# Token-form products over 512 columns of weights instead of 256, in a transformer kernel on one NeuronCore

## The reference

```python
proj = h @ w_in[l]                       # of it: hi, the values of the recurrence
x = x + g1 * (concat([o_a, o_b, o_c]) @ w_out[l])
# second block, layer i
h = x @ w_in                             # of it: c_q, c_kv and the values of attention
x = layer_norm(DEEPNORM_ALPHA * x + mix @ w_out, ln1_g[i], ln1_b[i])
x = layer_norm(DEEPNORM_ALPHA * x + swiglu(x, ...), ln2_g[i], ln2_b[i])
x = x + sigmoid(x @ ple_w_gate[i] + ple_b_gate[i]) * (p[i] @ ple_w_proj[i])
```

## Time and profile before

| | |
|---|---|
| median of 3 runs | 1397.43 us (1397.06 to 1399.79) |
| the profiled execution | 1398.54 us, of which the span 1396.7 us |
| TensorE busy | 1190.8 us, 85% of the span, 8196 matmuls |
| VectorE busy | 767.4 us, 55% |
| ScalarE busy | 531.9 us, 38% |
| bytes read | 198.70 MB, 143 GB/s over the span |

### The profile page before, as it was taken

How to read it: one execution, slowest core, us unless ns; L and a number is a source line. 1 busy time by engine, 2 the same in 40 slices (tenths; PEclk the granted TensorE clock), 3 DMA queues, 4 the chain that set the end, 5 groups by cost and what they waited for, 6 DMA issues and landing times.

```text
span 1396.7 us, 19126 instructions
## 1 busy us (share of the span) xinstructions
PE 1190.8 (85%) x8196; PEld 1078.1 (77%) x8196; DVE 767.4 (55%) x969; ACT 531.9 (38%) x705; POOL 0.2 (0%) x4
## 2 busy tenths in 40 slices
PE   4889872847999997975879999977999889999966
PEld 2788871437999886973679998867987589999866
DVE  3652459255777435547475665465443466666374
ACT  4541311143443333356443333333454443333332
POOL 0000000000000000000000000000000000000000
PEclk7799987768999998997799999989999889999988
DMA  9430323802455554420125555524531034555530
GB/s 387 188 136 30 109 103 121 352 10 91 159 183 188 195 185 168 169 93 1 50 105 183 185 188 193 183 67 183 189 121 61 5 141 150 187 183 181 186 116 31
DMA packets 28275, 200.97 MB, mean 144 GB/s; under 512 B 3104, under 2 KB 3616, under 8 KB 5024
## 3 DMA queue, kind: packets, MB, share of 16 engines
q1 hardware_dynamic: 26624, 190.30, 37.2%
q10 hardware_dynamic: 1568, 9.46, 1.8%
HBM read 198.70 MB, written 1.05 MB: 143 GB/s over the span
## 4 chain that ended last, share of the span: by engine, by line
PE 71%; DVE 16%; ACT 6%; DMA 4%; issue 3%; DVEq 0%; SPq 0%; ACTq 0%
PE bank L523 21%; PE bank L528 20%; PE bank L529 20%; DMA raw<-wstream 4%; DVE w_lo L1363 3%; PE bank L675 2%; PE bank L712 2%; DVE hT_lo L1381 2%; PE bank L668 1%; DVE hT_hi L1380 1%; PE bank L921 1%; PE bank L920 1%; PE bank L603 1%; DVE x_res L1826 1%; ACT w_hi L1013 1%
## 5 line engine op out<-in xcount | busy, mean ns | idle before, releaser
L1363 DVE TENSOR_TENSOR w_lo<-raw,w_hi 128x2048 fp32r<-128x2048 f32 (+1 forms) x159 | 357.9, 2257 | 180.0 <-ACT w_hi L1013 170.5
L1013 ACT ACTIVATE w_hi<-raw 128x2048 fp32r<-128x2048 f32 (+1 forms) x159 | 299.8, 1886 | 356.3 <-PE bank L523 304.3
L523 PE MATMUL bank<-hT_hi,w_hi 128*128 128x256 f32 (+1 forms) x1360 | 393.5, 289 | 22.0 <-DVE w_lo L1363 17.2
L528 PE MATMUL bank<-hT_lo,w_hi 128*128 128x256 f32 (+1 forms) x1360 | 390.4, 287 | 0.0
L529 PE MATMUL bank<-hT_hi,w_lo 128*128 128x256 f32 (+1 forms) x1360 | 389.9, 287 | 0.0
L523 PEld LDWEIGHTS bank<-hT_hi,w_hi 128*128 128x128 f32 (+1 forms) x1360 | 265.2, 195 | 27.2 <-DVE w_lo L1363 18.7
L528 PEld LDWEIGHTS bank<-hT_lo,w_hi 128*128 128x128 f32 (+1 forms) x1360 | 265.3, 195 | 0.2
L529 PEld LDWEIGHTS bank<-hT_hi,w_lo 128*128 128x128 f32 (+1 forms) x1360 | 265.1, 195 | 0.2
L523 PE MATMUL bank<-w_hi,hT_hi 128*128 128x256 f32 (+2 forms) x544 | 161.8, 297 | 31.3 <-DVE w_lo L1363 19.2
L528 PE MATMUL bank<-w_lo,hT_hi 128*128 128x256 f32 (+2 forms) x544 | 159.5, 293 | 0.0
L529 PE MATMUL bank<-w_hi,hT_lo 128*128 128x256 f32 (+2 forms) x544 | 159.1, 292 | 0.0
(11 more groups left out here) (252 smaller groups left out, 1080.6 us busy)
## 6 DMA issues: line engine op xcount, KB each, us to landing
raw<-wstream SPq DMA_DIRECT2D x179, 1024.0 KB, 4.8
arena<-prow ACTq DMA_DIRECT2D x2, 2560.0 KB, 11.2
x_res<-x ACTq DMA_DIRECT2D x1, 1024.0 KB, 15.2
rows<-prow ACTq DMA_DIRECT2D x2, 512.0 KB, 23.8
out<-x_res SPq DMA_DIRECT2D x1, 1024.0 KB, 4.0
const_sb<-const ACTq DMA_DIRECT2D x1, 872.0 KB, 19.3
raw<-wstream SPq DMA_DIRECT2D x1, 768.0 KB, 4.5
raw<-wstream SPq DMA_DIRECT2D x1, 544.0 KB, 3.8
```

Of the source, the lines that this page charges most:

```text
L523: ins = mm(o, a[0], b[0], start=start, stop=False)
L528: mm(o, a[0], b[1], start=False, stop=False)
L1013: A(w_hi[n % HI][:, 0:m], raw[:, slot % RAW, 0:m], ACT.Copy).then_inc(weights_rounded, 1)
L1363: V.tensor_tensor(w_lo[slot][:, 0:m], raw[:, slot, 0:m], w_hi[n % HI][:, 0:m].bitcast(F32), ALU.subtract).then_inc(weights_split, 1)
```

## The change

For hi, wo0, wo1, cqkv, sbv, fv0, o and pg the two tiles of a product are cut another way. Each now holds 512 rows of weights (four chunks k) by all 512 columns: tile .0 holds k 0 to 3, tile .1 k 4 to 7. The data in device memory stay as they were, and each transfer picks two runs of 1024 floats per partition, one from either old tile. Each matmul streams 512 columns, in two runs of 256 that lie 1024 apart. Block t of tokens has bank t to itself, and both banks are filled over both tiles: block 0 and block 1 over tile .0, then block 0 (bank 0 is then full) and block 1 over tile .1. `pp` also streams 512 columns, with a block of tokens to each bank. fv1, sv and kr stay.

Whoever empties a bank now takes 512 columns of one block in place of 256 columns of both. `add_attention` takes one statistic after each bank, where it took two after every second.

```diff
+WIDE = ["hi", "wo0", "wo1", "cqkv", "sbv", "fv0"] + [f"{n}{i}_{j}" for n in ("o", "pg") for i in range(2) for j in range(2)]
...
+                if name[:-2] in WIDE:
+
+                    j = int(name[-1])
+                    a, b = (TILE_NO[name[:-1] + c] for c in "01")
+                    sp.dma_start(raw[:, i % RAW, :].rearrange("p (j n) -> p j n", j=2),
+                                 wstream[a:b + 1:b - a, :, j * 1024:(j + 1) * 1024].rearrange("j p n -> p j n"))\
+                        .then_inc(weights_loaded[i % RAW], 16)
...
             def gemm_token(name):
 
+
+                banks = [begin(name, t) for t in range(TT)]
                 for j in range(2):
-                    token_half(f"{name}.{j}", T, key=(name, j))
+                    wh, wl, first = tile(f"{name}.{j}")
+                    vh, vl = (w.rearrange("p (c k n) -> p k c n", c=2, k=4) for w in (wh, wl))
+                    for t in range(TT):
+                        for i in range(4):
+                            k = 4 * j + i
+                            x_ready(k)
+                            last = product3(banks[t][:, :], x_part(k, t * P, (t + 1) * P),
+                                            (vh[:, i, :, :], vl[:, i, :, :]), k == 0, k == DC - 1, first)
+                        if j == 1:
+                            last.then_inc(psum_full, 1)
...
-                for n_ in range(4):
-                    b = begin("pp", layer, n_)
+                for n_ in range(2):
                     for t in range(TT):
+                        b = begin("pp", layer, 2 * n_ + t)
                         for k in range(2):
...
-                    xs = x[:, :, q * T:(q + 1) * T]
-                    done(V.scalar_tensor_tensor(out=xs, in0=xs, scalar=ALPHA,
-                                                in1=b[:, :].rearrange("p (t n) -> p t n", t=2),
+                    xs = x[:, q % 2, q // 2 * 512:(q // 2 + 1) * 512]
+                    done(V.scalar_tensor_tensor(out=xs, in0=xs, scalar=ALPHA, in1=b[:, :],
                                                 op0=ALU.mult, op1=ALU.add), *key)
-                    if q % 2:
-                        for t in range(TT):
-                            last = bn_piece(t, q // 2)
+                    last = bn_piece(q % 2, q // 2)
```

More of the change, by code:

```diff
@@ L487, in _ @@
                         sp.wait_ge(psum_full, full("mod", int(before[3:]) // 2))
-                sp.dma_start(raw[:, i % RAW, 0:width(name)], wstream[i, :, 0:width(name)])\
-                    .then_inc(weights_loaded[i % RAW], 16)
+                if name[:-2] in WIDE:
[4 more added lines that the diff above has]
+                        .then_inc(weights_loaded[i % RAW], 16)
+                else:
+                    sp.dma_start(raw[:, i % RAW, 0:width(name)], wstream[i, :, 0:width(name)])\
+                        .then_inc(weights_loaded[i % RAW], 16)
             sp.wait_ge(x_done, 1)
@@ L939, in _ @@
                 pe.wait_ge(p_split, layer + 1)
-                for n_ in range(4):
-                    b = begin("pp", layer, n_)
+                for n_ in range(2):
                     for t in range(TT):
+                        b = begin("pp", layer, 2 * n_ + t)
                         for k in range(2):
                             a = k * T + t * P
-                            last = product3(b[:, t * T:(t + 1) * T], (hid2_hi[:, a:a + P], hid2_lo[:, a:a + P]),
-                                            (vh[:, k, n_ * T:(n_ + 1) * T], vl[:, k, n_ * T:(n_ + 1) * T]),
+                            last = product3(b[:, :], (hid2_hi[:, a:a + P], hid2_lo[:, a:a + P]),
+                                            (vh[:, k, n_ * 512:(n_ + 1) * 512], vl[:, k, n_ * 512:(n_ + 1) * 512]),
                                             k == 0, k == 1, first)
-                    last.then_inc(psum_full, 1)
+                        last.then_inc(psum_full, 1)
                 for i in range(2):
@@ L1190, in _ @@
                         b = bank_of(f"cqkv.{e}", "cqkv", e)
-                        A(xn[:, :, e * T:(e + 1) * T], b[:, :].rearrange("p (t n) -> p t n", t=2), ACT.Copy)
-                        for t in range(TT):
-                            last = A(xn[:, t, 512 + e * T:512 + (e + 1) * T], b[:, t * T:(t + 1) * T], ACT.Square,
-                                     accum_out=ssum[:, 2 * t + e:2 * t + e + 1])
+                        A(xn[:, e, 0:512], b[:, :], ACT.Copy)
+                        for i in range(2):
+                            last = A(xn[:, e, 512 + i * T:512 + (i + 1) * T], b[:, i * T:(i + 1) * T], ACT.Square,
+                                     accum_out=ssum[:, 2 * e + i:2 * e + i + 1])
                         done(last, "cqkv", e)
@@ L1205, in _ @@
                         b = bank_of(f"sbv.{j}", "sbv", j)
-                        done(A(v_b.rearrange("p (t n) -> p t n", t=2)[:, :, j * T:(j + 1) * T],
-                               b[:, :].rearrange("p (t n) -> p t n", t=2), ACT.Copy), "sbv", j)
+                        done(A(v_b[:, j * 512:(j + 1) * 512], b[:, :], ACT.Copy), "sbv", j)
                     for j in range(2):
@@ L1286, in fox_input @@
                             c = half * 512 + j * T
-                            done(A(v_c.rearrange("p (t n) -> p t n", t=2)[:, :, c:c + T],
-                                   b[:, :].rearrange("p (t n) -> p t n", t=2), ACT.Copy), n_, j)
+                            if half == 0:
+                                done(A(v_c[:, j * D:j * D + 512], b[:, :], ACT.Copy), n_, j)
+                            else:
+                                done(A(v_c.rearrange("p (t n) -> p t n", t=2)[:, :, c:c + T],
+                                       b[:, :].rearrange("p (t n) -> p t n", t=2), ACT.Copy), n_, j)
                         else:
```

25 lines of the change are left out of this document (11 added, 14 removed).

## The result

Over 20 runs each, the changed kernel took a median of 1406.68 us (1395.14 to 1410.65) and the kernel before 1398.38 us (1395.23 to 1405.28). The ratio is 1.0054, with a 95% interval of 1.0040 to 1.0068: slower by half a per cent, 12.7 us above the forecast of 1394.0 and outside its range. The runs of the changed kernel lie in two groups, 17 at 1405.5 to 1410.7 and three at 1395.1, 1401.5 and 1402.8. The profiled one took 1405.49 us, span 1403.7; the profiled one of before had a span of 1396.7.

A forecast was written before the change was run, and what follows sets the result against it. TensorE's stream of products was taken as the bound, three `product3` lines being 61% of the last chain. Gains of 7.86 and 2.0 less 6.44 of costs gave 3.4 us, from 1397.43 to 1394.0, range 1391.2 to 1397.8.

The forecast's parts named there:

- 7.86 + 2.0 - 6.44: Touched stages, in us: gain from pairing products, plus starts without stops, minus pauses and late ends; 3.4 gained.
- The new pauses lower the clock: Rival: pauses in wo, o and pg bring stretches at 0.50, 1.7 us each; 1395.7 to 1397.4 us; chance 0.17.
- The moving operand: Rival: in wide products, two runs of 256 columns cost 240 ns, not 226.7; 1401.9 us, slower; chance 0.08.
- The clock in o0: Rival: o0's start loses its stops and its granted 0.68 becomes 1.00; 1.2 us less, 1392.8; chance 0.17.
- Streaming: In the touched products at full clock, each pair of narrow products made one wide saves 13.3 ns; 7.86 us in sum.
- wo, cqkv, fv0: Net stage forecasts: wo 0.72 us lost, cqkv 1.00 gained, fv0 0.64 gained.
- The five pauses: TensorE idle for a low half: 1.2 us between wo0 and wo1, 1.12 in each o, 0.54 in each pg.
- The late ends: Last bank emptied late behind a low half: 0.96 us at wo1's end, 0.88 at each end of o0 and o1.
- pg0: Stage pg0: 1.12 us from pairs at full clock less 0.54 of idle TensorE, a net gain of 0.58.
- pg1: Stage pg1: 1.18 us from pairs at full clock less 0.54 of idle TensorE, a net gain of 0.64.
- The wait behind `pp`: TensorE's 3.68 us wait for the next tile's low half covers the 0.32 us saved in `pp`; 0.3 longer.
- The order of VectorE that it named as the cost: VectorE empties bank 0, makes the next low half, then waits for bank 1; low half starts 3 us later than before.

The follow-up runs named there:

- e8: Changed kernel plus 40 extra rounded products (128x256, result unused) in layer 1's attention, four per unit from the seventh on; 1395.54 us, ratio 0.9979 against the kernel before.
- e14: Kernel before with four memsets on VectorE behind fv0, for which TensorE waits ahead of layer 1's attention; 1409.44 us, ratio 1.0071.
- e2: Kernel before with fv0 alone in the wide form; 1396.78 us, ratio 0.9997, nine runs at 1393.4 to 1398.6 and three at 1406.1 to 1411.9.
- e11: The kernel of e5 measured once more; 1386.41 us, ratio 0.9934, ten of 12 runs at 1383.1 to 1390.1, two at 1399.3 and 1399.6.
- e4: Changed kernel with 28 memsets on VectorE ahead of the splits of layer 1's input, delaying that layer; 1403.87 us, ratio 1.0034 against the kernel before.
- e5: Changed kernel with the next product's low half made before the wait for bank 0, in wo, o and pg; 1385.92 us, ratio 0.9911 against the kernel before.
- e9: Kernel before with the same 40 extra products in layer 1's attention as e8; 1401.41 us, ratio 1.0019.

## Why the prediction was wrong

**The step that failed** is in the sum: 7.86 + 2.0 - 6.44 was taken off the time of before with all untouched stages taken as they were, a term put at nothing without a reason. One of them, the attention of layer 1, took 11.03 us more, at a granted clock of 0.51 for 47.6 us where it had gone to and fro between 0.5 and 1. Without that the profiled run would have had a span of 1392.7, against the 1393.3 that was forecast, but this nearness is luck: the touched stages gave 1.8 us of the 3.4, and 2.2 came from other untouched ones. That the clock is the cause is shown by the windows (the same 236 matmuls, one pair at 1.15 us for 0.63) and by e8 (same arrival, same fall, extra products, no loss). What sends a run to the one state or the other is only narrowed down: both forms reach a long one (e14), one program comes out at either of two times (e2, e11), delays change the odds (e4 for the better, e14 for the worse), and neither the arrival nor the form of fv0 alone tells the outcome. In the traces without filler in which fv0 was wide, four of eight had a stretch of 37 us or more, and none of the seven in which it was narrow, the longest there being e14's 27; the traces are too few, and their kernels differ in too much, to make a rule of that.

**The rivals.** "The new pauses lower the clock" was the nearest, but had the wrong place and size: behind the pauses no stretch at 0.50 follows (the windows below, behind all five); it was priced at 1.7 us a fall near them, and the fall that cost came 128 us behind the nearest one, in a stage that has none.

```profile
329.30:341.00 11.70, 9.72 (x43) 1.00 0.52 179
697.30:709.50 12.20, 9.77 (x44) 1.00 0.50 173
943.00:956.00 13.00, 9.94 (x44) 1.00 0.48 161
1136.00:1148.00 12.00, 9.43 (x42) 0.99 0.46 170
1382.00:1392.00 10.00, 10.00 (x45) 1.00 0.00 0
```

"The moving operand" is refuted at 226.4 ns. "The clock in o0" came true beside the forecast: o0 gained 1.70 us and not 0.62, its start being granted 1.00 where the earlier trace rows had 0.68. I gave slower a chance of 0.08, all of it on the moving operand; no rival had an untouched stage getting slower, though the earlier trace rows showed stretches at 0.50 whose cause I could not name, and TensorE's products in attention were never looked at.

**The terms.** Streaming: right, 13.3 ns for each pair. wo, cqkv, fv0: within 0.3 us. The five pauses: 4.95 us in the trace, 4.52 forecast. The late ends: there, and e5 recovers them. pg0 (0.4 less than forecast) and pg1 (1.8 less) miss by the clock at their starts, 12 and 14 wide products at 0.53; the forecast counted pairs at full clock behind such a start, and took the start itself as unchanged. sbv: 0.62 for 0.64. The wait behind `pp` grew from 3.68 us to 4.10 in layer 0, where 0.3 more were forecast, and from 4.74 to 5.50 in layer 1. hi: 0.12 for 0.25. The wide tiles' transfers, taken as hidden, stayed so: the median landing is 4.9 us for the 4.8 of the earlier trace rows.

**The forecast's own repair works.** The order of VectorE that it named as the cost, changed in three lines, brings 1385.92 and 1386.41 us in two measurements, 0.9911 (0.9896 to 0.9925) and 0.9934 (0.9911 to 0.9957): the wide form is worth having, with the low half made before the wait for bank 0.

## What to carry to other kernels

When a bank is full later than before and nearer to the next one, look at what its reader does between the two, and move what others wait for ahead of the wait. And a sum over the touched stages is a forecast of those alone: in a stage where TensorE is the bound and the granted clock goes to and fro, look at its windows first, give its turning into one long low stretch a price (here 11 us) and a chance, and judge a change of under 1% by many runs and by stage, not by one median.

## What was not expected of the hardware

- TensorE can be in flight without a gap for 37.4 us and keep a granted clock of 0.51 (e2), with fp32 matmuls of 128x256 and 64x256 and transposes. With forty rounded products of 256 columns among them the low clock lasted 6.7 us where it had lasted 47.6, and the kernel was 11 us faster (e8), while they cost 3 us where the stretches were short (e9).
- In that attention the low clock comes with TensorE fully busy (6.80 of 6.80) and the full one with pauses (9.01 of 10.10). This does not show that a busy engine lowers the clock: the same matmuls at half the clock fill their pauses by themselves. It shows that the low clock can stand there without idle time of the engine.
- A moving operand in two runs of 256 columns, 1024 apart, streams at 226.4 ns, like a contiguous one of 512 (226.7).
